# Five changes of order in the instruction queues of a two-block transformer kernel

## The reference

```python
# first block
h = rmsnorm(x, g_mix);  z = h @ w_in            # 1024 -> x_rnn, g_rnn, q, k, v, gate_a, gate_b
xc = causal_conv(x_rnn);  hr = rg_lru(xc, ...)  # gated linear recurrence over the tokens
y_a = (hr * gelu(g_rnn)) @ w_rnn_proj
y_b = sliding_window_attention(q, k, v, ...) @ w_attn_proj   # 16 heads, window 128, sinks
x = x + (sigmoid(gate_a) * y_a + sigmoid(gate_b) * y_b) @ w_out
x = x + square(relu(rmsnorm(x) @ w_up)) @ w_down
x = x + (p @ w_ple_proj) * sigmoid(rmsnorm(x) @ w_ple_gate)
# second block
z = rms_norm(h) @ w_in_2                        # q_lat (384), kv_lat (256), k_rope (32), u_pool (512), 2 gates
q = rms_norm(q_lat) @ w_q_up_2;  kv = rms_norm(kv_lat) @ w_kv_up_2
# ... latent attention, pooling branch, cross attention to mem (w_xq_2, w_xkv_2, w_xo_2),
# ... a mixture of 32 experts with top-2 routing, and a final norm
```

## Time and profile before

| | us |
|---|---|
| median of 3 runs | 984.22 (984.15 to 984.26) |
| profiled execution, its own time | 984.22 |
| its span in the trace | 982.4 |
| TensorE busy (share of the span) | 966.8 (98%) |
| VectorE busy | 542.9 (55%) |
| ScalarE busy | 475.9 (48%) |

### The profile page before, as it was taken

The page is one execution under the profiler, slowest core; times in us unless marked ns, Lnnn a source line. Parts: engine busy times, 40 slices in busy tenths (PEclk is TensorE's granted clock), DMA queues, the critical chain, the costliest instruction groups (busy, mean ns, idle before and its releaser), DMA issues.

```text
span 982.4 us, 13615 instructions
## 1 busy us (share of the span) xinstructions
PE 966.8 (98%) x5479; PEld 740.7 (75%) x5479; DVE 542.9 (55%) x875; ACT 475.9 (48%) x761; POOL 0.8 (0%) x8
## 2 busy tenths in 40 slices
PE   9999999999999999999999999999999999999995
PEld 8878887887789888998889887889874455455442
DVE  5888896674666555545677874765372112112114
ACT  5588655756345544443665765454353223222222
POOL 0000000000000000000000000000000000000000
PEclk9999999999999999999999999999999999999998
DMA  9935465525455455554454743494289999999992
GB/s 295 321 129 172 172 214 171 172 87 172 159 172 204 171 172 172 201 206 152 141 166 158 253 131 129 136 321 146 92 316 337 394 395 392 395 392 396 391 397 108
DMA packets 107268, 223.53 MB, mean 228 GB/s; under 512 B 10185, under 2 KB 15042, under 8 KB 107202
## 3 DMA queue, kind: packets, MB, share of 16 engines
q1 hardware_dynamic: 104752, 219.10, 63.3%
q10 hardware_dynamic: 2450, 3.51, 1.2%
HBM read 221.54 MB, written 1.05 MB: 227 GB/s over the span
## 4 chain that ended last, share of the span: by engine, by line
PE 97%; DVE 1%; ACT 1%; issue 0%; POOL 0%; DVEq 0%; ACTq 0%; POOLq 0%
PE pb L461 21%; PE pb L463 21%; PE pb L462 21%; PE pb L2367 11%; PE pb L2390 6%; PE pb L2342 3%; PE pb L2405 3%; PE pb L524 2%; PE pb L595 1%; PE pb L544 1%; PE pb L664 1%; PE pb L2316 1%; PE pb L578 1%; PE pb L687 1%; PE pb L695 1%; PE pb L917 1%
## 5 line engine op out<-in xcount | busy, mean ns | idle before, releaser
L1468 DVE TENSOR_TENSOR wl<-raw,wh 128x2048 fp32r<-128x2048 f32 (+2 forms) x113 | 248.7, 2209 | 97.7 <-ACT wh L937 97.4
L937 ACT ACTIVATE wh<-raw 128x2048 fp32r<-128x2048 f32 (+2 forms) x114 | 208.4, 1836 | 113.8 <-PE pb L463 105.1
L461 PE MATMUL pb<-wh,th 128*128 128x512 f32 (+2 forms) x620 | 247.8, 400 | 0.0
L463 PE MATMUL pb<-wh,tl 128*128 128x512 f32 (+2 forms) x620 | 241.5, 390 | 0.0
L462 PE MATMUL pb<-wl,th 128*128 128x512 f32 (+2 forms) x620 | 241.3, 389 | 0.0
L461 PE MATMUL pb<-th,wh 128*128 128x256 f32 x544 | 156.4, 288 | 0.2 <-DVE wl L1932 0.2
L463 PE MATMUL pb<-th,wl 128*128 128x256 f32 x544 | 153.5, 282 | 0.0
L462 PE MATMUL pb<-tl,wh 128*128 128x256 f32 x544 | 153.2, 282 | 0.0
L461 PEld LDWEIGHTS pb<-wh,th 128*128 128x128 f32 x620 | 116.7, 188 | 27.0 <-issue 4.1
L463 PEld LDWEIGHTS pb<-wh,tl 128*128 128x128 f32 x620 | 116.6, 188 | 25.5
L462 PEld LDWEIGHTS pb<-wl,th 128*128 128x128 f32 x620 | 116.9, 188 | 22.7
(11 more groups left out here) (372 smaller groups left out, 1088.3 us busy)
## 6 DMA issues: line engine op xcount, KB each, us to landing
raw<-in_w_in SPq DMA_DIRECT2D x31, 1024.0 KB, 5.0
raw<-in_w_up SPq DMA_DIRECT2D x16, 1024.0 KB, 5.7
raw<-in_w_down SPq DMA_DIRECT2D x16, 1024.0 KB, 4.9
raw<-in_w_exp_gate SPq DMA_DIRECT2D x20, 512.0 KB, 9.8
raw<-in_w_exp_up SPq DMA_DIRECT2D x20, 512.0 KB, 11.6
raw<-in_w_exp_down SPq DMA_DIRECT2D x10, 1024.0 KB, 13.8
raw<-in_w_xkv SPq DMA_DIRECT2D x8, 1024.0 KB, 5.1
mwh<-in_w_exp_gate SPq DMA_DIRECT2D x14, 512.0 KB, 10.6
```

What stands on the lines that cost most here:

```text
L461: PE.matmul(o, lh, rh, start=start, stop=False, skip_group_check=True)
L463: return PE.matmul(o, ll, rh, start=False, stop=stop, skip_group_check=True)
L937: ACTE.activation(hi_of(i), raw_of(i), ACT.Copy).then_inc(S["hi"], 1)
L1468: DVE.tensor_tensor(lo_of(i), raw_of(i), hi_of(i).bitcast(F), ALU.subtract).then_inc(S["lo"], 1)
```

## The change

Five places, all of them order; no instruction is added or dropped.

1. The spreading of the first 1/rms row goes from the middle of unit ("x", 1, 0) to just behind the parameter transposes ahead of that unit; ScalarE copies it out before, not after, the exponential of the `lambda` chain.
2. ScalarE splits the unit behind `act_unit("gates", 1, 0)` after `act_gelu_square(3)` and `act_gates("gates", 0)`, no longer ahead of them.
3. Two `pe_scores` go from event 5 to event 6 of their unit.
4. VectorE's order in the attention: splits of weight units go ahead of `dve_masked`.
5. VectorE splits one unit of block two's start ahead of `dve_turn("q")`, which is no longer cut in two.

```diff
@@ pe_main
-            def row_x():
-                PE.wait_ge(*scaled("x"))
-                pe_row(rsx, 1)
-
             for b in range(2):
                 for r in range(2):
-                    pe_features(("x", b), r, 2, 0, turned("x") if b == 0 else None, {2: row_x} if (b, r) == (1, 0) else ())
+                    pe_features(("x", b), r, 2, 0, turned("x") if b == 0 else None)
...
                     PE.transpose(PB[0][:, 128:137], S0[0:9, 128:256], ident[0:9, 0:9]).then_inc(S["cols_mm"], 1)
+                    PE.wait_ge(*scaled("x"))
+                    pe_row(rsx, 1)
...
-                      (1, 0): {0: lambda: pe_values(0, 1), 2: lambda: pe_scores(2, 0), 5: lambda: pe_scores(2, 1)},
+                      (1, 0): {0: lambda: pe_values(0, 1), 2: lambda: pe_scores(2, 0), 6: lambda: pe_scores(2, 1)},
...
-                      (2, 0): {0: lambda: pe_values(1, 1), 2: lambda: pe_scores(3, 0), 5: lambda: pe_scores(3, 1)},
+                      (2, 0): {0: lambda: pe_values(1, 1), 2: lambda: pe_scores(3, 0), 6: lambda: pe_scores(3, 1)},
@@ act_main
+                    ACTE.wait_ge(S["row_mm"], 1)
+                    ACTE.activation(RSB, PB[1][:, 0:256], ACT.Copy).then_inc(S["row"], 1)
                     ACTE.wait_ge(S["lam_abs"], 1)
                     ACTE.activation(l1, l0, ACT.Exp, scale=-1.0).then_inc(S["lam_exp"], 1)
-                    ACTE.wait_ge(S["row_mm"], 1)
-                    ACTE.activation(RSB, PB[1][:, 0:256], ACT.Copy).then_inc(S["row"], 1)
...
             act_turn_k()
-            act_unit("gates", 1, 0)
             act_gelu_square(3)
             act_gates("gates", 0, (S["kq_mm"], 2))
+            act_unit("gates", 1, 0)
             act_gelu_tanh(2)
@@ dve_main
             dve_turn("mem", range(4, 8), "mem_norm_g_2", 0, banks=(2, 3))
+            dve_unit("w_rnn_proj", 1, 1)
             dve_masked(1, 0)
-            dve_unit("w_rnn_proj", 1, 1)
+            dve_probs(0)
+            dve_unit("w_xkv_2", 0, 0)
             dve_masked(1, 1)
-            dve_probs(0)
             dve_max(1)
-            dve_unit("w_xkv_2", 0, 0)
             dve_gated("w_rnn_proj", 1, 1, GA)
...
                 if n < 3:
                     dve_masked(n + 1, 0)
                 dve_probs(n)
+                dve_unit("w_xkv_2", n, 0)
                 dve_values(n - 1, 1)
                 if n < 3:
                     dve_masked(n + 1, 1)
                     dve_max(n + 1)
-                dve_unit("w_xkv_2", n, 0)
                 dve_unit("w_xkv_2", n, 1)
...
-            dve_turn("q", range(2), "q_norm_g_2", 1, banks=(2, 3))
             dve_unit("lat", 1, 1)
-            dve_turn("q", (2,), "q_norm_g_2", 1, banks=(2, 3))
+            dve_turn("q", range(3), "q_norm_g_2", 1, banks=(2, 3))
```

## The result

| | before | changed |
|---|---|---|
| median | 984.24 us | 996.69 us |
| ratio, 95% interval | | 1.0128 [1.0116, 1.014] |
| all executions recorded | 983.4 to 985.0 | 995.64 to 999.11 (33) |
| profiled execution, its own time | 984.22 | 997.38 |
| span of the profiled execution | 982.4 | 995.5 |

The medians are of four executions of each kernel, taken beside each other; the median of all 33 of the changed kernel is 996.93. The forecast was 994.4 us, in a range of 990.0 to 997.5. The change made the kernel 12.45 us slower; 10.2 were forecast. The lines of the changed kernel are numbered 3 lower from the removed helper on: its L1616 is L1619 of before, and so on.

A forecast was written before the change was run, and what follows sets the result against it. TensorE, busy 98% of the span, sets the time, so its waits are paid in full. 0.1 + 1.56 + 7.34 + 1.16 = 10.2 us on 984.22 gives 994.4 us; own range 992 to 996.5, 8 in 10 990.0 to 997.5.

The forecast's parts named there:

- Edit 1: First 1/rms row: TensorE waits some 0.2 us for the factors and saves a 0.1 us restart, +0.1 us.
- Edit 2: Gates block 2: the later split delays VectorE's low part, so TensorE begins at 126.42, +1.56 us.
- The cover of 0.3 us for the next unit: Gates: next low part ends at 131.6, TensorE asks at 132.0; if this fails, some tenths more.
- Edit 3: Scores at event 6: VectorE reaches them only after the split put ahead of them, so nobody waits; nothing.
- Edit 4: Attention: VectorE's splits delay the mask additions, +2.94 us in group 0, +2.20 each in groups 1 and 2, together +7.34.
- the wait at the scores: Group 0: late mask additions hold TensorE's overwriting of the score banks, +1.53 us, included in that group's +2.94.
- The 2.20 us steps: Groups 1 and 2: one split ahead of the second mask addition delays TensorE's transposes by +2.20 us each.
- Edit 5: The q latents: a 2.20 us split ahead delays TensorE's third transpose, +1.16 us (0.9 to 1.4).
- No giving back: Late in the kernel: the expert weights' stream starts as much later, so the delay isn't given back.
- the one on the clock: New waits of 1.2 to 2.2 us might drop TensorE to half clock; rival at 0.06, 997 to 1000 us.
- a dip of the clock before the end: Sign of being wrong: TensorE's granted clock dips before the end of the new trace.
- The price of a fall: After a long wait, each 3 us of work done at half clock adds 3 us.

The follow-up runs named there:

- e2: Kernel before, with only ScalarE's split in the gates moved behind two waiting pieces of ScalarE: 985.85 us, ratio 1.0025.
- e10: Kernel before, with only ScalarE's split in the gates moved, and 3 matmuls of constants put into TensorE's one resulting wait: 986.18 us, ratio 1.0019.
- e9: Changed kernel with matmuls of constants, products unused, put into all five long waits of TensorE in block one: 994.05 us, ratio 1.0096.
- e1: Kernel before, with only VectorE's new order in the attention and the scores at event 6: 991.81 us, ratio 1.0084.
- e3: Kernel before, with only VectorE's split of one unit put ahead of all of the q latents' split: 985.43 us, ratio 1.0014.
- e6: Kernel before, with VectorE's new attention order only in the loop over n, and the scores at event 6: 990.17 us, ratio 1.0065.
- e4: Kernel before, with only the first 1/rms row and ScalarE's copy of it moved: 984.07 us, ratio 1.0001.
- e7: Changed kernel with 8 matmuls of constants put into each of TensorE's two longest waits, in head groups 1 and 2: 996.94 us, ratio 1.013.

## Why the prediction was right, and where it was short

**What bounds the kernel.** Right. The edits showed in the time only as TensorE's waits and what these do to its clock; the same instructions took the same time on the other engines (VectorE 542.9 us busy before, 543.4 after).

**Edit 1.** Sized at +0.1, with 0 to +0.3 as bounds. Alone it is 0.15 us in the trace and nothing in the time; in the changed kernel's trace it is 0.58, outside the bounds. The term assumed that TensorE and the factors keep their distance of before; they don't from one trace to another.

**Edit 2.** +1.56 forecast, 1.57 in the changed kernel's trace. The chain came as worked out: ScalarE's high part behind its waiting piece, VectorE's low part at 124.07 (forecast 124.03), TensorE at 126.42 (forecast 126.42). But that agreement to 0.01 us is partly luck: the step is 1.89 in e2 and e10 and 2.06 in e9, where TensorE was 0.4 to 0.7 us ahead of the kernel before and waited longer for a low part that did not come earlier by as much. By the medians it is 1.7 (e2, falls included) and 1.8 (e10). The cover of 0.3 us for the next unit held, since no wait is printed there.

**Edit 3.** Nothing, as said: the changed kernel's trace prints no wait for it. It was not run alone.

**Edit 4.** +7.34 forecast, 7.2 in e1 and in the changed kernel. In group 0 the parts are further off than the total: the wait at the scores cost 1.81, not 1.53, and the one at the transposes 1.00, not 1.41. The total hangs on VectorE's chain alone, which came as worked out; the transposes started 0.15 us behind the mask addition, not the 0.26 taken, hence 2.81 for 2.94. The 2.20 us steps are exact because both ends of the distance, from the exponentials to the transposes, hang on TensorE's own progress and had no slack.

**Edit 5.** +1.16 forecast, 1.16 in the changed kernel and 1.17 in e3.

**No giving back.** Right: in e3 the shift at 718 us is that at 536 us.

**The sum is short by 2.3 us, and the step that failed is the one on the clock.** The prediction put a fall at 6 in 100 and the waits' length "between" what rows before could show; then it left the fall out of the forecast. It had also named a dip of the clock before the end as a sign of being wrong, and that sign came. The waits were worked out well: with the clock kept up (e9) the kernel takes 994.05 us, the forecast to 0.4 us. The rest is the falls. The profiled execution has two, none of the 33 took less than 995.64, 1.5 us above the slowest of e9, and 32 of the 33 have a mean clock of 0.991 to 0.995 (one 0.996, at 995.97 us). That the time still lies in the range of 8 in 10 is in part luck: its upper end, 997.5, stands 1.0 us above the forecast's own range without a working of its own. The price of a fall was mis-sized as well, 3 us. That matmuls start twice as far apart was right, but a stretch lasts 3.4 us in all, and 1.5 to 1.6 us of it are lost. The warning of the Trainium skill ("TensorE: Matmul & The Clock Gate", section "Why this matters for your kernels"), that idle gaps bring the half clock back, agrees with these traces in kind; the gaps after which it happened here, 2.1 to 2.3 us in the traces and by inference 1.6 in e2, are shorter than those that the page warns of, which the prediction's sentence on it didn't say. The measurement decides.

What stays open is why the same waits bring a fall in one execution and not in another (e1: one of five; e6: all five; e2: four of nine), and at which of the waits the falls of the timed executions lie, since only profiled ones show the place. Nor does the mean clock give the time: executions of the changed kernel with a mean clock of 0.992 took from 995.75 to 999.11 us. The single edits sum to 10.6 us (7.64 + 1.68 + 1.26 + 0.0, e1 to e4) and all together make 12.45; more falls per execution together would account for the difference, but their number per edit wasn't counted, so this is not shown.

## What to carry to other kernels

On an engine that takes its instructions in order, an independent bulk operation goes behind the short ones that the bounding engine waits for, and into the gap in which they have nothing to do; ahead of them it costs its full length each time round, however idle that engine is on average. To price a change of order, follow each moved instruction to the semaphore that the bounding engine waits on and compare it with that engine's arrival: in the changed kernel the delays of 1.2 to 2.9 us at the gates, the three head groups and the q latents came out within 0.15 us each (the gates up to 0.5 us off in other runs). Here waits of TensorE of 1.6 to 2.3 us cost some 1.5 us more by the clock in part of the executions; a few matmuls on constants that end before the wait does (e9) took that back.

## What was not expected of the hardware

- The clock fell after waits of 1.6 to 2.3 us (2.2 and 2.3 in the changed kernel, 2.1 in e6, by inference 1.6 in e2), in some executions and not in others. Waits up to 0.8 us (before) and 1.0 us (e3) left it at full.
- A stretch at the lower level lasted 3.41 us each time (two in the changed kernel's trace, one in e6's) and cost 1.5 to 1.6 us.
- A float32 matmul of 256 columns takes 0.43 us of TensorE, in two passes of 0.22 (e7); the three-pass products' matmuls of the same width start 0.12 us apart.
- From the end of a VectorE instruction to the start of the matmul that waits for it were 0.06 us in the changed kernel at line 461 (124.07 + 2.29 = 126.36 to 126.42) and at line 530, and 0.15 to 0.27 us at the transposes of line 595, where other waits came with it.
